# One-hots with four tokens side by side, and eight gathered rows and half of the last early low-part splits on the vector engine

## The reference, cut to what matters

```python
def peer_ffn(h, w_pq, sub_keys, peer_u, peer_v):
    ...
    e_idx = jnp.take_along_axis(cand_i, pos, axis=-1).reshape(T, PEER_HEADS * PEER_TOPK)
    gate = jax.nn.softmax(top_s, axis=-1).reshape(T, PEER_HEADS * PEER_TOPK)
    ...
        ub = jnp.take(peer_u, ib, axis=0).astype(jnp.float32)
        a = jnp.einsum('tkd,td->tk', ub, xb.astype(jnp.float32))
        a = jax.nn.gelu(a, approximate=False) * gb
        vb = jnp.take(peer_v, ib, axis=0).astype(jnp.float32)
        return jnp.einsum('tk,tkd->td', a, vb).astype(xb.dtype)
```

## Time and profile before

| | us |
|---|---|
| median of 3 runs | 3611.63 (3610.23 to 3613.88) |
| the profiled execution | 3612.62 |
| its span, from the first to the last instruction | 3610.8 |
| PE busy | 3423.8 (95%) |
| PEld busy | 3203.5 (89%) |
| DVE busy | 2209.9 (61%) |
| ACT busy | 992.8 (27%) |
| POOL busy | 1296.9 (36%) |
| granted TensorE clock, mean | 0.953 of 2.4 GHz |

### The profile page before, as it was taken

One profiled execution on the slowest core, in us unless ns is written; L12 is line 12 of the kernel. 1 busy time (PEld: TensorE's weight loads), 2 busy tenths in 40 slices (PEclk: granted clock), 3 DMA queues, 4 the chain that ended last, 5 costly groups with the idle time before them and its releaser, 6 DMA issues.

```text
span 3610.8 us, 61810 instructions
## 1 busy us (share of the span) xinstructions
PE 3423.8 (95%) x20514; PEld 3203.5 (89%) x20516; DVE 2209.9 (61%) x3937; ACT 992.8 (27%) x1823; POOL 1296.9 (36%) x871
## 2 busy tenths in 40 slices
PE   4999899898999999999989998989999999999998
PEld 3999879898999999987879997879999999999877
DVE  6498533785566557766246975348936655677662
ACT  3334323354322220011033343234542222200110
POOL 1333213378522333333113332124883233333330
PEclk7999999999988999999989999989998899999999
DMA  5477313245445897689635772123454469866994
GB/s 216 149 250 253 125 47 128 82 152 187 170 150 175 325 333 260 227 309 418 260 130 187 249 232 88 65 99 105 164 195 163 146 224 330 326 235 228 364 417 148
DMA packets 172874, 750.39 MB, mean 208 GB/s; under 512 B 19056, under 2 KB 23536, under 8 KB 138992
## 3 DMA queue, kind: packets, MB, share of 16 engines
q1 hardware_dynamic: 128304, 467.98, 37.5%
q0 software_dynamic: 36864, 268.45, 19.9%
q10 hardware_dynamic: 7616, 12.85, 1.1%
HBM read 745.53 MB, written 3.67 MB: 207 GB/s over the span
## 4 chain that ended last, share of the span: by engine, by line
PE 88%; DVE 4%; issue 3%; POOL 2%; ACT 2%; DMA 0%; ACTq 0%; DVEq 0%; POOLq 0%; SPq 0%
PE bank L696 26%; PE bank L505 16%; PE bank L506 16%; PE bank L510 16%; PE bank L688 10%; POOL split_lo L380 1%; PE bank L600 1%; PE bank L621 1%; ACT split_hi L375 1%; DVE h_lo L1165 1%; PE bank L654 1%; PE bank L526 0%; DVE waste L396 0%; PE bank L495 0%; DVE raw L396 0%
## 5 line engine op out<-in xcount | busy, mean ns | idle before, releaser
L380 POOL TENSOR_TENSOR split_lo<-raw,split_hi 128x1024 fp32r<-128x1024 f32 x306 | 790.1, 2584 | 1317.7 <-ACT split_hi L375 1317.1
L505 PE MATMUL bank<-h_hi,split_hi 128*128 128x256 f32 (+1 forms) x3712 | 1140.2, 325 | 67.1 <-DVE h_lo L1165 63.3
L506 PE MATMUL bank<-h_lo,split_hi 128*128 128x256 f32 (+1 forms) x3712 | 1116.8, 319 | 0.0
L696 PE MATMUL bank<-act_t,raw 128*128 (+1 forms) x4096 | 952.9, 389 | 5.7 <-DVE act_t L1527 2.6
L375 ACT ACTIVATE split_hi<-raw 128x1024 fp32r<-128x1024 f32 x512 | 543.1, 1061 | 1435.1 <-PE bank L510 1162.8
L696 PEld LDWEIGHTS bank<-act_t,raw 128*128 128x128 f32 x4096 | 784.8, 195 | 137.8 <-issue 33.3
L505 PEld LDWEIGHTS bank<-h_hi,split_hi 128*128 128x128 f32 x3712 | 745.5, 201 | 87.2 <-DVE h_lo L1165 79.8
L506 PEld LDWEIGHTS bank<-h_lo,split_hi 128*128 128x128 f32 x3712 | 750.4, 202 | 1.7
L510 PE MATMUL bank<-h_hi,split_lo 128*128 128x256 f32 (+1 forms) x3712 | 627.1, 312 | 25.7 <-POOL split_lo L380 25.7
L510 PEld LDWEIGHTS bank<-h_hi,split_lo 128*128 128x128 f32 x3712 | 575.2, 197 | 29.3 <-POOL split_lo L380 29.3
L380 DVE TENSOR_TENSOR split_lo<-raw,split_hi 128x1024 fp32r<-128x1024 f32 x206 | 258.5, 1255 | 552.8 <-ACT split_hi L375 552.4
(11 more groups left out here) (173 smaller groups left out, 2440.9 us busy)
## 6 DMA issues: line engine op xcount, KB each, us to landing
raw<-panels SPq DMA_DIRECT2D x768, 512.0 KB, 3.4
mod_raw<-mod_panels SPq DMA_DIRECT2D x96, 512.0 KB, 4.4
raw<-mod_panels SPq DMA_DIRECT2D x16, 512.0 KB, 5.3
bias<-bias_in ACTq DMA_DIRECT2D x16, 256.0 KB, 2.6
rowbuf<-rows,row_ring POOLq DMA_INDIRECT x256, 7.9
silu_c<-c_in SPq DMA_DIRECT2D x3, 1024.0 KB, 5.4
dft<-dft_in ACTq DMA_DIRECT2D x2, 1152.0 KB, 6.1
subk<-sub_keys ACTq DMA_DIRECT2D x2, 1024.0 KB, 6.7
```

The lines of the kernel that those rows point to most:

```text
L380: eng.tensor_tensor(col(split_lo, s % 2, D), col(raw, slot, D), col(split_hi, s % 2, D).bitcast(F32), ALU.subtract).then_inc(lo_ready[s], 1)
L505: mm(out, w_hi, rhs(rhs_hi, kk), start=(kk == 0), stop=False)
L506: mm(out, w_hi, rhs(rhs_lo, kk), start=False, stop=False)
L696: m = mm(col(bank[4 + kk // 2], kk % 2, TD), col(col(raw, s, D), kk, P), act_t[:, bass.ds(act_at * TD, TD)], start=False, stop=last and kk ...
```

## The change

- **Layout of the one-hots.** The 8 tokens of a batch lie in two halves of 4 (`SIDE`): within a half the four tokens are innermost. The matmuls now read both operands with a step of 4 elements. The vector engine's comparisons have the half as an outer loop; the multiplication with the gate is issued once for each half, so twice a batch. `index` is half as long.
- **The last four early groups (12 to 15).** The vector engine makes the low parts for odd `s` and runs a prompt row for each even `s`: 8 low parts, 8 rows. GpSimd makes the low parts for even `s` alone and starts a gather behind each of them. ScalarE makes a coefficient ahead of the high part at each even `s`.
- **The gating turns** have one prompt row each (at `u == 0`) in place of two. 16 rows lie ahead of the mixed turns as before, and the mixed and plain turns and the rest have the same rows as before.
- The gating turns of the vector engine and GpSimd are written out where they were loops, and the vector engine waits for the gelu of all 64 early panels ahead of the first one-hots, not between the first and the second.

```diff
 BATCH = 8
+SIDE = 4
...
+SHARED_G = EARLY_G - 4
+EARLY_ROWS = 2 * (EARLY_G - SHARED_G)
+GATING_ROWS = HALF // 4
+MIXED_ROWS = EARLY_ROWS + GATING_ROWS
...
                 for t in range(BATCH):
-                    w = col(hot2, u % 2, BATCH * P).rearrange("p (j t) -> p t j", t=BATCH)[:, t, :]
-                    parts = col(hot1, u % 2, BATCH * PARTS * CHUNK).rearrange("p (j t) -> p t j", t=BATCH)[:, t, :]
+                    seat_of = lambda h: h.rearrange("p (g j t) -> p g t j", g=BATCH // SIDE, t=SIDE)[:, t // SIDE, t % SIDE, :]
+                    w = seat_of(col(hot2, u % 2, BATCH * P))
+                    parts = col(hot1, u % 2, BATCH * PARTS * CHUNK)
                     for c in range(PARTS):
-                        last = mm(col(bank[2 + u % 2], t, CHUNK), w, col(parts, c, CHUNK), start=(c == 0),
+                        last = mm(col(bank[2 + u % 2], t, CHUNK), w, seat_of(col(parts, c, BATCH * CHUNK)), start=(c == 0),
                                   stop=(c == PARTS - 1))
...
-            def early(i):
+            def early(i, shared=False):
                 for s in range(SLOTS):
+                    if shared and s % 2 == 0:
+                        coefficient((i - SHARED_G) * 2 + s // 2)
                     split_panel_hi(l, *ahead(i + FIRST["peer"], s))
                     gelu(i + FIRST["peer"], s, i * SLOTS + s)
...
-            with pool.Fori(rows_from, EARLY_G) as i:
+            with pool.Fori(rows_from, SHARED_G) as i:
                 early(i)
...
+            for i in range(SHARED_G, EARLY_G):
+                for s in (0, 2):
+                    split_panel_lo(pool, l, *ahead(i + FIRST["peer"], s))
+                    m = (i - SHARED_G) * 2 + s // 2 + AHEAD
+                    gather(m, m % RING)
+
+            for w in range(HALF):
+                n, u = w // SLOTS, w % SLOTS
+                if u % 2 == 0:
+                    split_panel_lo(pool, l, *ahead(n + (FIRST["peer"] + EARLY_G), u),
+                                   at=u_seat(l, 0, u - 2) if w >= HALF - 2 else None)
+                if u == 0:
+                    m = EARLY_ROWS + n + AHEAD
+                    gather(m, m % RING)
...
+            def shared(i):
+                for s in range(SLOTS):
+                    if s % 2:
+                        split_panel_lo(dve, l, *ahead(i + FIRST["peer"], s))
+                    else:
+                        m = (i - SHARED_G) * 2 + s // 2
+                        prompt_row(m // RING, m % RING)
+
+            dve.wait_ge(h0_ready, l + 1)
+            carry(dve)
+            dot_row(0, 0)
+            for i in range(SHARED_G, EARLY_G - 2):
+                shared(i)
+            carry(dve)
             dve.wait_ge(route_stored, (l + 1) * DENSE)
...
+            for i in range(EARLY_G - 2, EARLY_G):
+                shared(i)
...
+                shape = [P, PARTS, CHUNK, SIDE]
+                for g in range(sides):
+                    last = V.tensor_tensor(
...
+                        .unsqueeze(2).broadcast_to(shape), ALU.mult)
+                last.then_inc(hot1_ready[u % 2], 1)
...
-            dve.wait_ge(h0_ready, l + 1)
+            dve.wait_ge(gelu_ready, l * NK + CHUNK)
             carry(dve)
-            dot_row(0, 0)
...
+            for w in range(HALF):
+                n, u = w // SLOTS, w % SLOTS
+                one_hots(0, n, u)
+                if w:
+                    gate_acts(0, (w - 1) // SLOTS, (w - 1) % SLOTS)
+                if u == 0:
+                    m = EARLY_ROWS + n
+                    prompt_row(m // RING, m % RING)
+                if u % 2:
+                    split_panel_lo(dve, l, *ahead(n + (FIRST["peer"] + EARLY_G), u),
+                                   at=u_seat(l, 0, u - 2) if w >= HALF - 2 else None)
             gate_acts(0, HALF_G - 1, SLOTS - 1)
```

127 lines of the change are left out of this document (52 added, 75 removed).

## The result

The changed kernel takes 3403.98 us (median of 4 runs, 3401.12 to 3406.33), the kernel before 3611.47: a ratio of 0.9424, 95% interval 0.9408 to 0.9441, 207 us less. The profiled execution took 3406.3 us, with a span of 3404.2.

A forecast was written before the change was run, and what follows sets the result against it. TensorE, partly through its low clock, was taken to bound gating and plain, with stepped operand reads setting the gate group's time. 2 x (55 + 51 - 3) = 206 us off 3612.6 gave 3406.6, put at 3410; range 3370 to 3482.

The forecast's parts named there:

- The step of 8 becomes 4: Gate matmuls: halving the operands' step makes a matmul 61 ns instead of 122, a group 1.46 us instead of 2.94.
- the step was not it: Rival, gate matmuls: instruction issue sets the 122 ns, so nothing shortens; 3618 to 3632 us, slower; chance 0.07.
- half of it: Rival, gate matmuls: 80 to 94 ns each, groups of 1.95 to 2.26 us; 3452 to 3480 us; chance 0.15.
- more than that: Rival, gate matmuls: 30 to 41 ns each, groups of 0.7 to 1.0 us; 3362 to 3376 us; chance 0.15.
- Plain: Plain stage: a unit takes 5.0 us, the stage 156.5 against 212, 55 us less a layer.
- The bound by the vector engine: Plain stage: with matmuls of 30 ns the vector engine would limit a unit to 4.85 us.
- Gating: Gating stage: a unit takes 5.2 us, the stage 164 against 215, 51 us less a layer.
- The wait of 2.5 us in each turn: Gating turns: TensorE waits behind ScalarE's high part, GpSimd's split, the row's dot and one-hots; 0.6 us a unit.
- the first wait: Way into gating: TensorE waits 1.7 us for the first one-hots, in place of 1.4 us at the second group.
- The last 16 early panels: Last early panels: added rows and low parts cost 3 us more a layer, at most 10.
- The term of 6.2 us for two panels: Last early panels: vector engine and GpSimd's shared path takes 6.2 us against TensorE's 5.76, 0.4 over for each of 8 pairs.
- The vector engine keeps its rate: One-hots: assumed no slower on runs of 4; the rival has the rate lost, 3536 to 3570 us, chance 0.05.

The follow-up runs named there:

- e_step: Changed kernel, gate matmul weights read every 8 bytes, columns every 32 in gating and every 4 in plain: groups 2.85 and 0.80 us.
- e_unit: Changed kernel with both gate matmul operands read every 4 bytes in gating and every 2 in plain: groups 0.74 and 0.70 us.
- e_allsplit: Changed kernel with all low parts of a gating turn on the vector engine, none on GpSimd: 3390.6 us, ratio 0.9387.
- e_dot: e_allsplit with the next row's dot product moved two units behind the row's add in gating: 3362.2 us, ratio 0.9304.
- e_shared: Changed kernel with the old layout of eight tokens side by side, so only rows and splits move: 3621.4 us, ratio 1.0025.
- e_layout: Kernel before with only the new layout of four tokens side by side; rows and splits stay: 3407.4 us, ratio 0.9432.
- e_norows: e_layout with all gating low parts on the vector engine and the next row's dot one unit behind the add: 3382.2 us, ratio 0.9357.
- best: e_dot with early rows one group earlier and the first one-hots between the two splits of the last early group: 3355.6 us, ratio 0.9292.

## Why the prediction was right, and where it was not

- **The time.** 3410 was forecast and 3404 measured; the terms were 55 + 51 - 3 a layer, and 55.7 + 46.4 + 0 and 1 in mixed came. The two sums are both 103 a layer, and that they agree so closely is luck: gating came 4.6 short, and the early panels and mixed made up for it.
- **The step of 8 becomes 4.** 61 ns a matmul were forecast, 1.48 us a group came, and 242 and 118 ns for matmul and load, as written. The rule behind it, time in proportion to the bytes stepped, is right only between 4 and 16 bytes: 32 bytes cost no more than 16, and 2 bytes hardly less than 4 (0.70 and 0.74 us). It gave the right number because the two steps of this change lie in that stretch. That both operands have to be read faster was not so: the columns decide, and the weights' 16 bytes cost 0.05 to 0.12 us a group. The rivals "the step was not it", "half of it" and "more than that" fell with the 1.48 us. The Trainium skill's 81 ns for a load and a matmul ("TensorE: Matmul & The Clock Gate", section "Back-to-back issue gap") are for 128 columns and no bound for this pair of 64: it took 62 ns here, and 31 to 33 at 4 bytes.
- **Plain.** 156.5 us forecast and measured, with a clock of 1.00. TensorE is busy in all of it, so the 0.08 us by which a unit is longer than 4.92 are its own. The bound by the vector engine, 4.85 us a unit, was right too: `e_step` and `e_unit` found it at 148.7 us, 4.8 a unit.
- **Gating.** The wait of 2.5 us in each turn is there, at the place and from the terms named, 2.51 and 2.52 us; `e_unit`, `e_allsplit` and `e_dot` bear the chain out. One link ran the other way round: the prediction lets the row's dot wait for GpSimd's split, and in the turns the split waits for the dot and then holds the comparison. As these run one after another, the sum is the same. From the first group 31 x 5.2 + 1.5 = 162.7 was forecast, 164.1 and 163.0 came. The step that failed is the first wait: 1.7 us forecast, 4.95 measured (5.2 by the tables). The prediction has the vector engine's split done 0.2 us before TensorE is ready and the one-hots 1.9 later. The split was done 0.7 us after it, because it stood behind a dot that ran beside GpSimd's split; and the one-hots took 4.2 us, because they too ran beside a split of GpSimd. The second part, 2.3 us, is the exclusion that the prediction used elsewhere and left out here; `e_allsplit`, without that split, has 3.0 in place of 5.2.
- **The last 16 early panels.** 3 us more a layer forecast, nothing came. The term of 6.2 us for two panels was too high: a row's dot and GpSimd's split beside it take 3.42, and two panels 5.69, from one dot's start to the next, of TensorE's 5.76. So the vector engine keeps pace, but has no time left in which to make the first one-hots ahead of the stage, as the kernel before did (925.37 in the earlier trace rows). That falls due as the first wait. 3 + 1.7 forecast for the two and 0 + 5.2 measured nearly cancel, by luck.
- **What the prediction did not ask** is what the move of the rows does by itself. It put the 51 us of gating down to the change as a whole. All of it is the layout's: at 2.94 us a group the move is worth nothing (`e_shared`), and at 1.48 us in this order it is worth what it costs (`e_layout` against the change). It is worth 23 to 27 us only in an order that the change does not have.
- **The vector engine keeps its rate** on runs of 4: that rival fell too. 0.34 and 0.60 us from start to start for the comparisons, as before, and 1.01 us for the two halves of the third where one instruction had taken 0.95.

## What to carry to other kernels

Read an operand's step in bytes against its recorded time before anything else is moved: here the layout was the whole gain. Where TensorE waits for another engine, shorten TensorE's own part in a test: if the turn does not shrink, the other engines set it. A second test, with more load on them or another order, tells which of the two it is: here moving half of a row by two units was worth 28 us, and moving eight rows to another stage nothing. Before work is taken out of a stage for the sake of its transfers, cut the stage where its work changes and look at the distance of the starts: a mean rate over the whole of it, and a busy share of overlapping matmuls, both hide what holds it.

## What the runs showed of the hardware that I had not expected

- **The clock falls beside long groups without any wait.** Gating has 0.83 in `e_shared` and 0.86 in `e_step` (group 2.85), where TensorE waits only for the first group; with groups of 1.48 us and waits of at most 0.7 us (`e_norows`, `best`) it has 1.00. With the short groups it fell only behind longer waits: the changed kernel has 0.94, and 0.50 in the stretch behind its first wait. Before, the low clock had cost a layer's gating some 30 us (215.0 less 31 x 5.84, a last group of 2.9 and one wait of 1.5), and most of that came back with the layout; the prediction's unit of 5.2 has only falls behind waits in it. The stage in `e_norows`:

```profile
935.00:1097.00 162.00, 146.63 (x1530) 140.97 (x1530) 148.76 (x228) 51.85 (x98) 64.21 (x36) 1.00 0.60 214
```

- **Who waits, GpSimd's split or the vector engine's instruction, is not the same everywhere.** In the last early panels the split goes first (2.58 us, the dot 3.42), in the gating turns the dot (1.22 us, the split 3.80), though the split is recorded from ahead of the dot in both. Why is open.
- **Whether a group follows the clock depends on the step.** At 16 bytes a group takes the same time whatever the granted clock, and at 8 too: the first group of the changed kernel has 0.50 and 1.46 us to the next matmul. At 4 bytes it does not: `e_unit`'s groups behind a wait take 1.25 us, in a stretch with a clock of 0.60, and the others 0.90 at 1.00. The first stretch is of the changed kernel, the two below of `e_unit`:

```profile
948.70:949.90 1.20, 1.20 (x22) 1.20 (x23) 1.20 (x2) 0.00 (x0) 0.77 (x1) 0.50 1.00 416
```
```profile
1035.70:1036.80 1.10, 1.10 (x25) 1.10 (x25) 1.10 (x2) 0.00 (x0) 0.68 (x1) 0.60 0.82 317
1040.90:1041.60 0.70, 0.70 (x26) 0.70 (x25) 0.69 (x2) 0.57 (x1) 0.00 (x0) 1.00 0.95 387
```
